# The normed x of a two-layer hybrid trunk begins 8 bytes off a multiple of 16 in SBUF

## The reference

```
h = rms_norm(x, pre_mix_norm)              # x * rsqrt(mean(x^2)) * gain
p = h @ w_in                               # 2048 x 5648: q, k, v, z, xbc, dt
A = causal attention(q, k, v), 8 heads of 128; S = Mamba-2 chunked scan(xbc, dt), 16 heads of 64
y = concat(rms_norm(A), group_rms_norm(S * silu(z))) @ w_out      # 2048 x 2048
x = x + rms_norm(y, post_mix_norm)
h = rms_norm(x, pre_mlp_norm)
x = x + rms_norm(relu(h @ w_up)^2 @ w_down, post_mlp_norm)        # 2048 x 8192, 8192 x 2048
```

## Time and profile before

| what | value |
|---|---|
| median of three runs | 2222.07 us |
| the profiled execution | 2221.54 us, its span 2219.8 us |
| granted TensorE clock, mean | 0.998 |
| PE busy | 2193.4 us (99%), 12256 matmuls |
| PEld busy | 1918.4 us (86%), 12256 weight loads |
| DVE, ACT, POOL busy | 1353.8 us (61%), 1012.4 us (46%), 113.5 us (5%) |
| HBM | 182 GB/s over the span |

### The profile page before, as it was taken

The page is one execution under the profiler, slowest core; times in us unless marked ns, Lnnn a source line. Parts: engine busy times, 40 slices in busy tenths (PEclk is TensorE's granted clock), DMA queues, the critical chain, the costliest instruction groups (busy, mean ns, idle before and its releaser), DMA issues.

```text
span 2219.8 us, 33955 instructions
## 1 busy us (share of the span) xinstructions
PE 2193.4 (99%) x12256; PEld 1918.4 (86%) x12256; DVE 1353.8 (61%) x1592; ACT 1012.4 (46%) x1280; POOL 113.5 (5%) x115
## 2 busy tenths in 40 slices
PE   9999999999999999999999999999999999999997
PEld 9999888888888888888899988888888888888886
DVE  7877464764555465556578774657555655554655
ACT  6443464543444344344454445546434434443443
POOL 2141000000000000000001410000000000000000
PEclk9999999999999999999999999999999999999999
DMA  7555556656666656665645555665666566666564
GB/s 217 152 169 153 162 189 199 181 177 204 185 196 194 190 183 197 194 188 191 191 127 162 164 159 154 198 196 171 198 192 191 177 207 178 201 190 194 178 202 164
DMA packets 208556, 405.96 MB, mean 183 GB/s; under 512 B 12540, under 2 KB 12820, under 8 KB 207956
## 3 DMA queue, kind: packets, MB, share of 16 engines
q1 hardware_dynamic: 206660, 398.04, 58.6%
q10 hardware_dynamic: 1264, 5.31, 0.7%
q0 software_dynamic: 544, 1.38, 0.3%
HBM read 402.58 MB, written 2.10 MB: 182 GB/s over the span
## 4 chain that ended last, share of the span: by engine, by line
PE 65%; issue 31%; DVE 2%; ACT 1%; DMA 0%; POOL 0%; POOLq 0%; DVEq 0%; ACTq 0%
PE wide L792 11%; PE wide L724 10%; PE wide L726 10%; PE wide L725 10%; PE wide L800 6%; PE wide L759 4%; PE wide L762 4%; PE wide L761 4%; DVE xbcT L1263 1%; PE wide L914 1%; DVE x_sb L1196 1%; PE wide L827 0%; PE wide L935 0%; DVE w_lo L1114 0%; DMA wk<-in_ssd_out_norm 0%
## 5 line engine op out<-in xcount | busy, mean ns | idle before, releaser
L1114 DVE TENSOR_TENSOR w_lo<-raw,w_hi 128x1024 fp32r<-128x1024 f32 x755 | 924.8, 1234 | 742.7 <-ACT w_hi L481 740.8
L481 ACT ACTIVATE w_hi<-raw 128x1024 fp32r<-128x1024 f32 x755 | 791.6, 1058 | 966.5 <-PE wide L726 503.0
L724 PE MATMUL wide<-w_hi,u_hi 128*128 128x512 f32 x1280 | 498.5, 389 | 0.0
L726 PE MATMUL wide<-w_hi,u_lo 128*128 128x512 f32 x1280 | 498.0, 389 | 0.0
L725 PE MATMUL wide<-w_lo,u_hi 128*128 128x512 f32 x1280 | 497.9, 389 | 0.0
L792 PE MATMUL wide<-a_both,w_hi 128*128 128x512 f32 x2032 | 487.0, 391 | 0.0
L792 PEld LDWEIGHTS wide<-a_both,w_hi 128*128 128x128 f32 x2032 | 373.1, 188 | 72.0
L726 PEld LDWEIGHTS wide<-w_hi,u_lo 128*128 128x128 f32 x1280 | 240.3, 188 | 49.9
L725 PEld LDWEIGHTS wide<-w_lo,u_hi 128*128 128x128 f32 x1280 | 240.3, 188 | 49.7
L724 PEld LDWEIGHTS wide<-w_hi,u_hi 128*128 128x128 f32 x1280 | 240.3, 188 | 49.6
L800 PEld LDWEIGHTS wide<-a_both,w_lo 128*128 128x128 f32 x2032 | 260.7, 191 | 9.9
(11 more groups left out here) (235 smaller groups left out, 1263.7 us busy)
## 6 DMA issues: line engine op xcount, KB each, us to landing
raw<-in_w_up SPq DMA_DIRECT2D x256, 512.0 KB, 3.9
raw<-in_w_down SPq DMA_DIRECT2D x256, 512.0 KB, 4.3
raw<-in_w_in SPq DMA_DIRECT2D x179, 512.0 KB, 3.7
raw<-in_w_out SPq DMA_DIRECT2D x64, 512.0 KB, 4.3
zg<-in_post_mix_norm ACTq DMA_DIRECT2D x2, 1024.0 KB, 5.0
zg<-in_post_mlp_norm ACTq DMA_DIRECT2D x2, 1024.0 KB, 6.8
out<-x_sb SPq DMA_DIRECT2D x8, 256.0 KB, 2.5
x_sb<-in_x ACTq DMA_DIRECT2D x2, 512.0 KB, 7.0
```

The costliest lines, as they stand in the source:

```text
L481: act.activation(w_hi[:, c % RING], raw[:, c % RING], ACT.Copy).then_inc(sem["hi_ready"], 1)
L724: pe.matmul(o, sh, wh, start=(k == 0), stop=False)
L726: ins = pe.matmul(o, sl, wh, start=False, stop=(k == KT - 1))
L1114: dve.tensor_tensor(w_lo[:, c % RING], raw[:, c % RING], w_hi[:, c % RING].bitcast(F32), ALU.subtract).then_inc(sem["split_done"], 1)
```

## The change

The buffer of the normed x is declared as a flat room of 8192 + 128 words, and `a_both` is the part of it from word 2 to word 8193, seen in the same four-dimensional shape. All its addresses are 8 bytes higher, and each stretch of 256 or 512 words begins 8 bytes behind a multiple of 16. The room is 512 bytes longer than the contents; by the declarations the buffers behind it keep their distance from a multiple of 512. No instruction is added or removed.

```diff
-        a_both = sb("a_both", [P, KT, 2, SEQ], F32R)
+
+        a_room = sb("a_room", [P, KT * 2 * SEQ + P], F32R)
+        a_both = a_room[:, 2:2 + KT * 2 * SEQ].rearrange("p (k a s) -> p k a s", k=KT, a=2)
         u_hi = sb("u_hi", [P, KT, SEQ], F32R)
```

## The result

The changed kernel takes 2232.28 us (median of four runs, 2231.73 to 2232.41) against 2221.99 us: the ratio is 1.0046, with a 95% interval of 1.0031 to 1.0061. It is 10.3 us slower. I had forecast no change.

What follows compares the result with a forecast made beforehand. The prediction took TensorE, busy 99% of the span, to bound the kernel through distances between matmul starts. Its four parts, each valued at 0, summed to no change: 2222 us, with an 8-in-10 range of 2175 to 2275 us.

Steps and rivals of the forecast that it cites:

- the case that I took for the likeliest: Whole kernel: no change, 2222 us, with its own range of 2218 to 2226; chance 0.33.
- That TensorE's distances are the whole time: TensorE, busy 99% of the span: time is a sum of distances between matmul starts, and only there can the change act.
- Part 1: Moving operand of 6864 matmuls at addresses 8 bytes higher: valued at 0 ns, as streaming stays contiguous and of equal length.
- two rival bounds: Moving operand, per matmul: lower bound -6.7 ns (-46 us), upper bound of the near rows +5 ns (+34 us).
- more clashes: Rival on TensorE: stream and load meet more often, 5 ns or more on 6864 matmuls, 34 us, 2256 us; chance 0.17.
- Part 2: Stationary operand, 3 x 256 weight loads in token_chunk: valued at 0, with -5 to +4 us possible through the surcharge.
- 37 ns of cover: Weight loads in token_chunk: about 190 ns beside a 227 ns stream, so about 37 ns more would stay covered.
- Part 3: ScalarE's 64 writes and VectorE's 64 writes and reads back: valued at 0, at most 0.3 us, nearly all beside TensorE's work.
- Part 4: Buffers behind the room, moved by 512 bytes: offsets within 16, 32 and 512 kept, wdt_both's 16-byte offset too; value 0.
- a small fixed extra: Rival between the 6864 matmul starts: one more memory unit per stretch, 3 to 11 us, 2225 to 2233 us; chance 0.16.
- fewer clashes: Rival on TensorE: surcharge drops as in the dt product, 46 to 51 us faster, 2171 to 2176 us; chance 0.25.
- Half rate: Rival on TensorE: offset moving operands stream at half rate, 970 us more, about 3190 us; chance 0.09.

Runs made afterwards that it cites:

- e1_room_only: Kernel before with the room 512 bytes longer but a_both at its first word: 2222.03 us against 2221.83, ratio 1.000.
- e2_a64: Kernel before with a_both beginning 64 bytes into the room: 2215.04 us, 7 us less than before.
- e6_a112: Kernel before with a_both beginning 112 bytes into the room: 2210.33 us, ratio 0.9948.
- the scan: Bench without the trunk: four matmul forms, normed x at 22 places from 0 to 480 bytes; at 112 bytes both 256-word forms took 113.3 ns.
- b1_offsets: Bench without the trunk: streams of 48 matmuls at varied load/move offsets; 512 words moving took 227 ns at 0/0, 233 at 0/8.
- The pairs: Load/move offset pairs of the bench of 48-matmul streams, one stretch moving repeatedly, trunk left out; 256 words took 120 ns at 0/0, 117 at 0/8.
- e4_w8: Kernel before with only w_hi and w_lo 8 bytes off: 2235.46 us.
- e7_a4: Kernel before with a_both beginning 4 bytes (one word) into the room: 2259.23 us.
- e5_wlo64: Kernel before with only w_lo 64 bytes farther: 2236.77 us.
- b3_forms: Bench without the trunk: four matmul forms at thirteen placements of w_hi, w_lo and normed x; all at 0 bytes took 120, 227, 226.7, 120 ns.

## Why the prediction was wrong

I had put the time at 2222 us and gave a slower kernel a chance of 0.39. The 2232 us lie inside my range of 2175 to 2275 but outside the 2218 to 2226 of the case that I took for the likeliest.

- **That TensorE's distances are the whole time, and that the change can act only there:** right. The table of distances accounts for the span to 0.1 us, and the longest waits didn't change.
- **Part 1, value 0 for the moving operand:** this is the step that failed. I had read from the earlier trace rows and from the earlier trace rows that the surcharge on a matmul isn't a constant, and then set its change to nothing because the stretch stays contiguous and of the same length. That argument is about the 106.7 ns of streaming; the change worked on the 13.3. Wide high paid 4.9 ns on each of 2032 matmuls (9.9 us), nearly the upper bound of rows 8 (5 ns); feature gained 1.2 ns on each of 2640 (-3.2 us). The small sum of 10 us is what is left of effects of both signs. Of the two rival bounds, +5 ns was near the truth for wide high; -6.7 was far off for feature. That one change could do both at once wasn't among the cases. And what spoke against "more clashes", that the stream "settles at 226.7 by itself", was just what the 8 bytes took away.
- **Part 2, the stationary operand:** bounded at -5 to +4 us, valued at 0, measured +2.0 us. The 37 ns of cover were beside the point: the loads still last 188 ns, and the distance is longer all the same.
- **A reading that mixes shapes:** "the step of one and the same shape goes from about 7 to about 18 ns over the streaming time" puts two shapes together. With 256 words the rows go from 6.7 to 13.3 ns, with 512 from 13.3 to about 18.
- **Part 3, the writes:** right. L510 467 for 464 ns and L1161 478 for 476, 64 each: 0.3 us of busy time off the path.
- **Part 4, the 512 bytes:** right, e1_room_only shows it. One thing I had put down by declared sizes was wrong: `wdt_both` isn't 16 bytes off a multiple of 32. Buffers are given starts rounded up to 32 bytes; it stands 64 bytes from `a_both` modulo 128 (bytes 216,256 and 82,048 in the built program). So the gain that I had ascribed to 16 bytes belongs to another place.
- **The rival "a small fixed extra"** had the total right (2225 to 2233 us) and the mechanism wrong: no fixed extra, for L802 pays next to nothing and L764 gains. **"More clashes"** is nearest for wide high alone (its 34 us assumed all forms), **"fewer clashes"** for feature. **Half rate** is excluded: no form of the changed kernel pays more than 7 ns on the mean distance.
- **The Trainium skill** was weighed at two places. "SBUF — State Buffer", section "SBUF: two separate sides", gives lines of 16 bytes. From these alone one would take multiples of 16 to be alike; e2_a64, e6_a112 and the scan show that they aren't. Its table in "Who interferes with whom" lets TensorE's two read ports be independent; in b1_offsets, with the move at 0, the load's place alone changes 120 to 115.6 (5.55/48) and to 113.3 ns. The measurement decides against reading that table as "the address of one can't matter".

**Shown:** the 8 bytes cause the 10 us; they act through the distance between starts of float32r matmuls, in the forms that read `a_both`, by amounts of both signs; it needs no other engine; and the places of the stationary and of the moving operand both count. **Shown in part:** that benches foretell whole kernels. The pairs came within about 2 us of e4_w8 (with terms that cancel) and e7_a4, missed e5_wlo64 by 31 us, and the scan gave e6_a112 twice its gain. b3_forms accounts for e5_wlo64, but for the place of e2_a64 it gives +8 us (wide high +13, token with x +5, feature -6, wide low -4) where -7 was measured. **Open:** what inside TensorE or its reads makes the surcharge. It isn't in proportion to the columns loaded, it isn't set by the offsets alone (L55 against L58, and L106 against L156), and no run here looks deeper.

## What to carry to other kernels

In a float32r kernel bound by TensorE, measure the distance between matmul starts against columns over clock; what is above it (here 13 of 120 and 227 ns) depends on where both operands lie in SBUF, and a scan of places with the kernel's real sequence of matmuls is worth its one run: here it gave 0.5%. Don't ask only whether a start is a multiple of 16. With 512 words moving, 4 bytes was the worst place tried (237 ns), but 8 bytes (233) was no worse than most multiples of 16, and only 0 and 256 kept 227 in both forms. Moving off them paid only where the gain with 256 words was larger. Don't carry a distance from one sequence or shape to another, and time the whole kernel: such sums missed once by 31 us, and once the kernel gave half the gain.

## What was unexpected in the hardware

- A float32r stream has a surcharge of 6.7 to 23 ns per matmul that goes with the operands' places (113.3 to 123 ns for 256 words, 226.7 to 237 for 512), where bfloat16 has 2.5 to 2.9 ns (109.2 to 109.6 and 215.8) at the four offset pairs tried.
- Places at 16, 64 and 112 bytes differ as much from 0 as 8 bytes do. For 384 words moving, 8 bytes changed nothing (8.33 and 8.32 us for 48).
- The same matmuls at the same addresses ran at 117 ns in one bench and at 120 in another, and the same form at the same place at 229 and at 233. Within one kernel, groups of one line took in turn 113 and 117.5 ns (e2_a64). What picks the distance is open.
- With 512 words moving, fewer columns loaded made the stream at 0/0 slower: 227.5 ns with 128 columns, 231.7 with 32.
